# Second attention in another order with two more buffers, and its output projection begun in its last steps

## The reference, cut to what matters

```python
def _swa_sinks(h, w_q, sinks, w_o, k_band, v_band):
    q = (h @ w_q).reshape(B, nc, CHUNK, KV_B, GROUP_B, HEAD_DIM)      # 16 chunks of 64, 16 heads of 64
    s = jnp.einsum('bnqgrd,bnkgd->bngrqk', q, k_band).astype(jnp.float32) / math.sqrt(HEAD_DIM)
    s = s - slopes[...] * dist[...]                                    # 128 keys for each chunk
    m = jnp.maximum(jnp.max(s, axis=-1, keepdims=True), sink)
    e = jnp.exp(s - m)
    denom = jnp.sum(e, axis=-1, keepdims=True) + jnp.exp(sink - m)
    p = (e / denom).astype(v_band.dtype)
    o = jnp.einsum('bngrqk,bnkgd->bnqgrd', p, v_band).reshape(B, S, H_B * HEAD_DIM)
    return o @ w_o
```

## Time and profile before

| | us |
|---|---|
| median of 3 runs | 2517.85 (2514.11 to 2519.14) |
| the profiled execution | 2521.02, span 2519.2 |
| PE busy | 2337.5 (93%) |
| DVE busy | 1536.2 (61%) |
| ACT busy | 1149.7 (46%) |
| POOL busy | 1172.5 (47%) |
| granted clock of PE, mean | 0.966 |

### The profile page before, as it was taken

How to read it: one execution, slowest core, us unless ns; L and a number is a source line. 1 busy time by engine, 2 the same in 40 slices (tenths; PEclk the granted TensorE clock), 3 DMA queues, 4 the chain that set the end, 5 groups by cost and what they waited for, 6 DMA issues and landing times.

```text
span 2519.2 us, 30443 instructions
## 1 busy us (share of the span) xinstructions
PE 2337.5 (93%) x10984; PEld 1932.2 (77%) x10984; DVE 1536.2 (61%) x2470; ACT 1149.7 (46%) x1933; POOL 1172.5 (47%) x1580
## 2 busy tenths in 40 slices
PE   4899999997989999999999898988899999999996
PEld 3778788886867777777778687776678888888884
DVE  4565656557777666666664766773375555444456
ACT  4365665748044333333333566662354333333334
POOL 3411313120646666666666351204356666666660
PEclk9989999999999999999999899978899999999998
DMA  6111211113821333333331321114111111111111
GB/s 259 52 47 34 68 34 54 47 47 102 316 76 58 117 118 114 122 121 118 118 105 57 111 68 40 51 34 175 42 34 51 51 51 51 63 55 52 58 51 67
DMA packets 66007, 206.91 MB, mean 82 GB/s; under 512 B 7345, under 2 KB 7985, under 8 KB 65730
## 3 DMA queue, kind: packets, MB, share of 16 engines
q1 hardware_dynamic: 29760, 109.06, 13.2%
q10 hardware_dynamic: 36098, 95.91, 11.6%
HBM read 186.66 MB, written 16.32 MB: 81 GB/s over the span
## 4 chain that ended last, share of the span: by engine, by line
PE 65%; DVE 14%; ACT 8%; POOL 4%; issue 4%; DMA 4%; ACTq 1%; DVEq 0%; POOLq 0%
PE bank L883 38%; PE bank L620 17%; POOL w_spl L549 2%; DVE X L1889 2%; PE bank L636 1%; POOL w_raw L556 1%; DVE H L1610 1%; PE bank L780 1%; PE bank L754 1%; PE bank L815 1%; PE bank L790 1%; POOL S3f L556 1%; PE bank L816 1%; PE bank L817 1%; DVE cV L1859 1%
## 5 line engine op out<-in xcount | busy, mean ns | idle before, releaser
L883 PE MATMUL bank<-H,w_spl 128*128 128x512 f32 x3744 | 880.6, 393 | 33.3 <-DVE H L1610 14.6
L883 PEld LDWEIGHTS bank<-H,w_spl 128*128 128x128 f32 x3744 | 704.3, 189 | 198.0 <-DVE X L1889 29.4
L549 POOL TENSOR_TENSOR w_spl<-w_raw,w_spl 128x256 fp32r<-128x256 f32 x688 | 544.9, 820 | 443.5 <-ACT w_spl L1358 442.1
L620 PE MATMUL bank<-H,w_spl 128*128 128x512 f32 x2016 | 520.7, 408 | 24.9 <-DVE H L1610 10.7
L883 PE MATMUL bank<-TB,w_spl 128*128 128x512 f32 x2112 | 492.5, 389 | 0.3 <-ACT sU L1373 0.3
L620 PEld LDWEIGHTS bank<-H,w_spl 128*128 128x128 f32 x2016 | 386.5, 197 | 106.4 <-issue 20.6
L883 PEld LDWEIGHTS bank<-TB,w_spl 128*128 128x128 f32 x2112 | 396.2, 188 | 83.4 <-issue 0.9
L1358 ACT ACTIVATE w_spl<-w_raw 128x512 fp32r<-128x512 f32 x328 | 201.9, 628 | 546.7 <-PE bank L883 332.9
L487 POOL TENSOR_TENSOR pace<-one_s 128x1 f32<-128x1 f32 x50 | 13.4, 267 | 737.6 <-PE bank L780 355.8
L1889 DVE SCALAR_TENSOR_TENSOR X<-bank,mods,X 128x1024 f32<-128x1024 f32 x176 | 225.0, 1279 | 34.2 <-PE bank L883 34.2
L1882 DVE TENSOR_TENSOR bank<-bank,sU 128x512 f32<-128x512 f32 x80 | 55.9, 699 | 299.7 <-PE bank L883 299.7
(11 more groups left out here) (171 smaller groups left out, 3186.5 us busy)
## 6 DMA issues: line engine op xcount, KB each, us to landing
w_raw<-in_w_stream SPq DMA_DIRECT2D x184, 512.0 KB, 3.8
ada_raw_f<-in_ada_t ACTq DMA_DIRECT2D x128, 256.0 KB, 2.9
ada_raw_o<-in_ada_t ACTq DMA_DIRECT2D x8, 2048.0 KB, 8.3
ada_raw<-in_ada_t SPq DMA_DIRECT2D x8, 1024.0 KB, 18.6
negF<-scratch_f ACTq DMA_DIRECT2D x16, 512.0 KB, 3.8
X<-in_x_t SPq DMA_DIRECT2D x4, 1024.0 KB, 10.8
X<-in_x_t ACTq DMA_DIRECT2D x4, 1024.0 KB, 8.1
scratch_x<-X ACTq DMA_DIRECT2D x1, 4096.0 KB, 12.6
```

Of the source, the lines that this page charges most:

```text
L549: last = pool.tensor_tensor(block_at(layer, b, 1, q, q + 256), src[:, q:q + 256], block_at(layer, b, 0, q, q + 256).bitcast(F32), ALU.subt ...
L620: last = pe.matmul(dst, stat(k, a), mov(k, b), start=(k == 0 and a + b == 0), stop=(k == KT - 1 and a == 1))
L883: last = pe.matmul(dst, block_at(layer, b, x, k * P, k * P + P), mov(y), start=(start and x + y == 0), stop=(stop and x == 1), skip_group_ ...
```

## The change

`PTB` and `O_stB` get a second buffer each, the store of a pair its own semaphores (`o_outB`), and the parts of a pass are put in another order:

- PE: scores of u, transposes of u-2, values of u-3, query quarter.
- DVE: maxima of u, low part of q, low part of the turned probabilities of u-2, normalising of u-1, output sum of u-3 (was u-4).
- ACT: high part of the turned probabilities, store, output half of u-3, exponentials of u, high part of q.

In the last passes ACT loads pairs back into `Hf`, the low half of H seen as float32 (`load_pair`: pairs 0 to 2 in pass 27, 3 and 4 in 28, 5 in 30, 6 in 33), and makes high parts (`pair_high`); DVE makes the low parts in place (`pair_low`), pair 0 in pass 28 up to pair 5 in pass 33. PE takes the sum over these pairs for the first projection tile in the same passes (`out_first`: k = 0 in pass 30 up to 3 in pass 33, 4 and 5 in 34). Behind the loop come k = 6 of the first tile, k = 0 to 6 of the second, and k = 7 of both (`out_two`). The banks of the projection tiles are swapped for this layer, so that the first tile uses banks that the values don't.

```diff
+PAIR_LOADS = {27: (0, 1, 2), 28: (3, 4), 30: (5,), 33: (6,)}
+PAIR_SPLITS = {28: (0,), 29: (1,), 30: (2,), 31: (3,), 32: (4,), 33: (5,)}
+OUT_BESIDE = {30: (0,), 31: (1,), 32: (2,), 33: (3,), 34: (4, 5)}
+PAIRS_BEHIND = [6, 7]
+OUT_BEHIND = [6]
...
-        PTB = at("PTB", [P, 2, 512], F32R, 182)
+        PTB = [at(f"PTB{i}", [P, 2, 512], F32R, kb) for i, kb in enumerate((182, 200))]
-        O_stB = at("O_stB", [P, S], F32, 190)
+        O_stB = [at(f"O_stB{i}", [P, S], F32, kb) for i, kb in enumerate((190, 204))]
...
+            def out_first(ks):
+                for k in ks:
+                    if k == 0:
+                        pe.wait_ge(w_ready, tile_order(W_OUT_B) + 1)
+                        pe.wait_ge(qB_lo, 16)
+                    pe.wait_ge(o_lo, 8 + k + 1)
+                    out_step(1, 0, k, int(k == 0))
+            def out_two():
+                out_first(OUT_BEHIND)
+                pe.wait_ge(w_ready, tile_order(W_OUT_B + 1) + 1)
+                pe.wait_ge(o_addB, 64)
+                for k in range(KT - 1):
+                    out_step(1, 1, k)
+                out_first([KT - 1])
+                out_step(1, 1, KT - 1, 1)
...
+                if 2 <= u <= 33:
+                    turn_b(u - 2)
                 if u >= 3:
                     values_b(u - 3)
-                if 2 <= u <= 33:
-                    turn_b(u - 2)
                 if u < 27:
                     q_quarter((u + 1) // 4 + 1, (u + 1) % 4)
-            out_proj(1)
+                out_first(OUT_BESIDE.get(u, ()))
+            out_two()
...
+            def load_pair(k):
+                if k == 0:
+                    act.wait_ge(qB_ps, 16)
+                for e in range(2):
+                    act.wait_ge(o_outB[k % 2][e], 16 * (k // 2 + 1))
+                act.dma_start(Hf[:, k, 1], dO[k]).then_inc(ob_in[k], 16)
+            def pair_high(k):
+                act.wait_ge(ob_in[k], 16)
+                nc.scalar.activation(H[:, k, 0], Hf[:, k, 1], ACT.Copy).then_inc(o_hi, 1)
...
+            send_pair(7)
+            for k in PAIRS_BEHIND[:-1][:2]:
+                pair_high(k)
+            load_pair(7)
...
+            for j in range(4):
+                act.dma_start(X[:, 2 * j:2 * j + 2], dX.rearrange("k p s -> p k s")[
+                    :, 2 * j:2 * j + 2]).then_inc(x_in[j], 16)
+            pair_high(7)
...
+            def pair_low(k):
+                dve.wait_ge(o_hi, 8 + k + 1)
+                V_.tensor_tensor(H[:, k, 1], Hf[:, k, 1], H[:, k, 0].bitcast(F32), ALU.subtract).then_inc(o_lo, 1)
```

More of the change, by code:

```diff
@@ L189, in program @@
         H = at("H", [P, KT, 2, S], F32R, 0)
+        Hf = at("Hf", [P, KT, 2, S], F32, 0)
         ada_raw0 = at("ada_raw0", [P, KT, 2, D], F32, 0)
@@ L356, in program @@
         o_in = [sem(f"o_in{i}") for i in range(4)]
+        o_outB = [[sem(f"o_outB{i}{e}") for e in range(2)] for i in range(2)]
+        ob_in = [sem(f"ob_in{k}") for k in range(KT)]
         o_hi = sem("o_hi")
@@ L973, in ffn @@
                 return used[0]
-            out_proj(0)
+            for m in range(8):
+                out_tile(0, m)
             square_sum(1, 1)
@@ L1052, in values_b @@
                     for part in range(2):
-                        last = pe.matmul(bank(4 + u % 2, j * P, j * P + P), v, PTB[:, part, j * P:j * P + P],
+                        last = pe.matmul(bank(4 + u % 2, j * P, j * P + P), v, PTB[u % 2][:, part, j * P:j * P + P],
                                          start=(part == 0), stop=(part == 1))
@@ L1069, in _ @@
                     pe.wait_ge(vs_in, 48)
+                if 2 <= u <= 33:
+                    turn_b(u - 2)
                 if u >= 3:
                     values_b(u - 3)
-                if 2 <= u <= 33:
-                    turn_b(u - 2)
                 if u < 27:
                     q_quarter((u + 1) // 4 + 1, (u + 1) % 4)
-            out_proj(1)
+                out_first(OUT_BESIDE.get(u, ()))
+            out_two()
+            for m in range(2, 8):
+                out_tile(1, m)
             square_sum(3, 1)
@@ L1820, in out_proj @@
                 gc = M_G1 + M_L1 * layer
-                for k in range(8 if layer else 0):
-                    dve.wait_ge(o_hi, 8 * layer + k + 1)
-                    V_.tensor_tensor(H[:, k, 1], O_raw[:, k % 4], H[:, k, 0].bitcast(F32),
-                                     ALU.subtract).then_inc(o_lo, 1)
                 for m in range(8):
@@ L1994, in _ @@
             dve.wait_ge(vs_in, 48)
-            for u in range(36):
-                if u <= 27 and u % 2:
-                    q_low(u // 4 + 1, u % 4 // 2)
+            def pair_low(k):
+                dve.wait_ge(o_hi, 8 + k + 1)
+                V_.tensor_tensor(H[:, k, 1], Hf[:, k, 1], H[:, k, 0].bitcast(F32), ALU.subtract).then_inc(o_lo, 1)
+            for u in range(35):
                 if u < 32:
@@ L2015, in _ @@
                     V_.tensor_scalar(nmB[:, b], mxB[:, b], sink_s[:, hp:hp + 1], -1.0, ALU.max, ALU.mult).then_inc(mB, 1)
+                if u <= 27 and u % 2:
+                    q_low(u // 4 + 1, u % 4 // 2)
+                if 2 <= u <= 33:
+                    v = u - 2
+                    dve.wait_ge(ptB_hi, v + 1)
+                    V_.tensor_tensor(PTB[v % 2][:, 1], bank(2 + v % 2), PTB[v % 2][:, 0].bitcast(F32),
+                                     ALU.subtract).then_inc(ptB_lo, 1)
                 if 1 <= u <= 32:
```

105 lines of the change are left out of this document (47 added, 58 removed).

## The result

The changed kernel takes 2476.8 us (median of 4 runs, 2475.8 to 2480.9), the kernel before beside it 2516.4 (4 runs, 2514.1 to 2519.1): a ratio of 0.9844 with an interval of 0.9826 to 0.9861, or 35 to 44 us less. The sign and the first part of the forecast held. Of the 8.2 us, 4.3 are the last steps and the projection, which gave more than was worked out; these alone would have left it inside the range, at 2480.7. The rest is the base, the clock at the start of the attention, and code that the change leaves alone.

What follows compares the result with a forecast made beforehand. PE was taken as the bound in the steady steps, not fully used because of waits and clock. 2521.02 less 23.0 (steady steps 21.9, start 1.1) less 9.7 (last steps) is 2488.3; median 3.2 lower, 2485; range 2480 to 2497.

Steps and rivals of the forecast that it cites:

- part 2: Step 27 (start T) to projection's end: six pairs' read-back and 24 projection matmuls move into the steps; 9.7 us gain.
- So I expect 1.2 GHz: Last steps, from 27: PE idles up to 2.5 us at a time, so half clock; values end at T+41.4.
- DMA issues on ACT cost 0.64 each: Last steps: each pair-load issue takes ACT 0.64 us; three in step 27, two in 28, one in 30.
- The slack: Odd steady steps: normalised probabilities are ready 5.35 us after step start, PE's transposes want them at 5.8; 0.4 us spare.
- The chain of high part, low part, maxima and exponentials: Last steps: maxima 1.2, exponentials 1.85, high part 1.06, low part 1.25, one after the other, 5.4 us a step.
- rival 1: Last steps: the clock comes back because each has 2.6 us of projection beside small matmuls; time 2481; chance 0.12.
- Pair 6 is there: Behind the last steps: pair 6's low part comes at T+46.8, when PE has finished pair 5.
- The 1.1 us of the start: Attention's start: DVE's maxima of step 1 move ahead of the low part of q; first normalising 1.1 us earlier.
- Rival 2: Steady steps: the transposes' 0.4 us slack fails, odd steps lose 0.7 to 0.9 us; time 2495; chance 0.12.
- Rival 3: Last steps: chain high-low-maxima is 7 us long, or pair 7 lands late; part 2 gives nothing, 2495; chance 0.06.
- Rival 4: Steady steps: late normalising stops all of PE and the clock falls, 7.7 us a step against 5.86; 2552; chance 0.04.
- Rival 5: Whole change: the order doesn't change anything that ends last; gain under 5 us; chance 0.04.

Runs made afterwards that it cites:

- the run with the large memset: Changed kernel plus a DVE memset of 1408 columns ahead of the normalising in steps 3 to 26: 2509.8 us, ratio 0.9974.
- the run with the small memset: Changed kernel plus a DVE memset of 256 columns (0.27 us) ahead of the normalising in steps 3 to 26: 2478.4 us.

## Why the prediction was wrong in the last steps, and where it was right

The steps that failed are two of part 2. "So I expect 1.2 GHz": the clock came back beside the projection's matmuls. "DMA issues on ACT cost 0.64 each": they ran beside the exponentials and delayed them by nothing. The end of the values, forecast at T+41.4, came at T+36.2. Of these 5.2 us, 2.0 had been won by the maxima of step 31 (T+23.9, forecast T+25.85): the six issues up to there were priced at 3.8, and 2.0 of waits for PE that the layout didn't have stand against them. The other 3.2 lie behind these maxima, in a stretch with a clock of 0.72 and not 0.50.

**What bounds, and the steady steps: right.** One step was laid out as 4.93 us of PE and taken as 4.95; it measured 4.96, 24 of them 119.0, as forecast, with no wait that makes a row and the clock at 1.00. The 18.5 us of waits that the prediction says would go reach to 1735 us; 11.3 of them lie in these steps, and the sum used 140.70 us as measured, so nothing hung on it. Without its own order DVE would have cost 5.4 us.

**The slack: right in most steps, used up in six.** The forecast had 0.4 us on an odd step. On the timeline of the changed kernel the normalising from 1596.93 ends at 1597.62 and the transposes start at 1598.01, 0.4 later. But in six of the 24 steps it is not 0.69 us long but 1.08:

```profile
1586.76 1.87 POOL L504 TENSOR_TENSOR w_spl<-w_raw,w_spl 128x256 fp32r<-128x256 f32 x2
...
1586.97 1.08 DVE L2070 TENSOR_TENSOR PB<-PB,rdB 128x512 f32<-128x512 f32 x1
...
1587.20 0.22 PE L1062 MATMUL bank<-KSB,QB 128*128 128x128 f32 x1
...
1588.10 0.44 PE L1073 MATMUL bank<-id_f,PB 128*128 128x128 f32 x2
```

It ends 0.05 us before the transposes, which is the hand-over of the run with the large memset and no margin. PE's rows of the step from 1597.16 show what an unhindered one looks like:

```profile
1597.16 0.22 PE L1062 MATMUL bank<-KSB,QB 128*128 128x128 f32 x1
...
1598.01 0.62 PE L1073 MATMUL bank<-id_f,PB 128*128 128x128 f32 x4
```

There the transposes start 0.84 us behind the first score. In the six steps, here from 1587.20, they start 0.90 to 0.92 behind it, and these steps are 5.03 to 5.06 us long where the other 18 are 4.93. So PE did stand for the normalising, by 0.06 to 0.07 us six times. The longer steps make 0.6 to 0.7 us in all, the difference between 119.0 and 24 x 4.93 = 118.3. A second row tells POOL's side, the split instruction of this line in steps 3 to 26 (ns, min/median/max, first and last start):

```profile
L504 POOL TENSOR_TENSOR w_spl<-w_raw,w_spl x24: 729/736/1178, 1527.2 to 1629.0; 128x256 fp32r<-128x256 f32 x24
```

In the run with the small memset the normalising starts 0.44 us after POOL's first split, not 0.21, and takes 0.85, not 1.08. In both it ends 1.29 us after POOL started: 0.69 of its own behind a wait until POOL + 0.60, near the end of a split of 0.73. And POOL's second split, which starts in that time, takes 1.18, longer by 0.45. So each seems to have stood for the other. By this, what the Trainium skill says in SBUF — State Buffer, section "SBUF: two separate sides", that the two exclude each other for a whole instruction, agrees with the trace in six steps of 24, to within some 0.15 us. Where the prediction erred was in the length of what excludes: it took the mean of 0.82 us in the earlier trace rows, which has such waits in it, where the undisturbed split is 0.73. And it let the wait begin with the normalising at its worst, where POOL had already begun 0.21 us before. The two nearly cancel: 0.39 us were lost in each of the six steps, where some 0.33 were free, 0.38 less the hand-over. That the cost was 0.6 us and not 2.5 is luck: POOL's split had begun 0.21 us ahead of the normalising, in each of the six.

**The last steps: the mechanism right, the size too small.** The forecast had T+125.4 for the end of the projection; it is T+121.1 and T+121.6. By its terms:
- "DMA issues on ACT cost 0.64 each": this step failed. The issues of pass 27 run beside the exponentials that stand ahead of them, on the timeline of ACT:

```profile
1645.27 0.40 ACT L1581 ACTIVATE PB<-PB,nmB 128x128 f32<-128x128 f32 x1
1645.38 0.33 ACTq L1552 DMA_DIRECT2D Hf<-scratch_o  x1
...
1645.80 0.41 ACTq L1552 DMA_DIRECT2D Hf<-scratch_o  x1
...
1646.31 0.39 ACTq L1552 DMA_DIRECT2D Hf<-scratch_o  x1
...
1646.83 0.28 ACT L1583 ACTIVATE esB<-nmB,sink_s 128x4 f32<-128x4 f32 x1
1648.15 0.60 ACT L1565 ACTIVATE PTB<-bank 128x512 fp32r<-128x512 f32 x1 [1.04 <-PE bank L1073]
```

  The exponentials took 1.84 us, as without issues, and ended at T+5.35, not T+7.75. Against that ACT then waited twice for PE, 1.04 and 1.00 us, which the layout didn't have. Net, the maxima of step 29 came at T+12.87, not at 14.6. The trace of before already showed it, at a store whose issues run beside exponentials that start 0.39 us apart as ever:

```profile
1691.01 0.45 ACTq L1528 DMA_DIRECT2D scratch_o<-O_stB  x1
1691.13 0.39 ACT L1544 ACTIVATE PB<-PB,nmB 128x128 f32<-128x128 f32 x1
...
1691.50 0.61 ACTq L1528 DMA_DIRECT2D scratch_o<-O_stB  x1
1691.52 0.39 ACT L1544 ACTIVATE PB<-PB,nmB 128x128 f32<-128x128 f32 x1
```

- The chain of high part, low part, maxima and exponentials: 5.4 us were forecast for a step, and the maxima of steps 29, 30 and 31 come at T+12.87, 18.17 and 23.88, that is 5.3 and 5.7 apart. DVE's rows show the chain, the low part waiting for ACT's high part and the maxima behind it:

```profile
1658.67 1.23 DVE L2034 TENSOR_TENSOR H<-Hf,H 128x1024 fp32r<-128x1024 f32 x1 [0.47 <-ACT H L1556]
1659.93 0.29 DVE L2050 CUSTOM_DVE_ANT_0 PB<-bank,bias_s 128x128 f32<-128x128 f32 x1
...
1663.99 1.62 DVE L2034 TENSOR_TENSOR H<-Hf,H 128x1024 fp32r<-128x1024 f32 x1 [0.45 <-ACT H L1556]
1665.64 0.29 DVE L2050 CUSTOM_DVE_ANT_0 PB<-bank,bias_s 128x128 f32<-128x128 f32 x1
```

- "So I expect 1.2 GHz": this step failed too, from 1661 on (T+19.4), and that was rival 1, to which I gave 12 in 100. It had in its favour the one row of before in which dense matmuls brought the clock back, and against it only rows that had none in them; the second kind says nothing of a mixture. The end of the values was forecast at T+41.4, and at T+37 if the clock came back; it is T+36.2 and 35.1.
- "Pair 6 is there": wrong, first for the same reason. With PE through sooner, it waited 2.54 us for it, where rival 1 said 3. Some 2 us of this wait are ACT's order (the high part behind the last store), which the layout didn't look at. Moving the second tile ahead gives the wait and more, 3.9 to 4.4 us.
- The rest of the projection was forecast at 84.0 us and took 84.9 with this wait in it, so 82.3 without; the slow start was gone with the clock.

5.2 us sooner at the values' end and 0.9 later behind it make the 4.3 us. The total for these steps hid another mistake, which didn't change it: the forecast laid the gain to the pairs alone, where a third or more of it (4.7 to 6.5 of 14.0 to 15.3 us) is the new order's.

**The start and the rest.** The 1.1 us of the start are neither borne out nor refuted. To step 3 the kernels with DVE's new order take 15.6 to 15.9 us in three executions, with a granted clock of 0.89 there, and 16.8 to 17.6 in the other eight, with 0.80 or 0.81; before it was 17.6 and 18.1, with 0.81. At the same clock the gain is 0 to 1.3 us, and most of the 2.1 in the table is clock. The base was one profiled execution whose last stretch was at the long end, 716.6 of 712.5 to 716.6; the forecast took it over, less the 3.2 us to the median. The median of before was itself 1.5 us lower with a fourth run. These are no part of the mechanism, and that they carried the time out of the range is chance.

**The rivals.** Rival 1 came true. Rival 2 did in a small way: the slack failed in six steps, by 0.07 us and not by 0.7 to 0.9. Rival 3: the chain was 5.3 to 5.7 us, not 7. Rival 4's mechanism is real, as 1.23 us more on DVE showed (2509.8 us, of the changed kernel's gain all but 6 us gone). Rival 5 is out.

**The range** ended 0.5 us under rival 1, at 2480. That rival was itself priced on a base and a start that were each some us too high, and on issues that cost more than they do; an end of the range should not stand on the value of one case.

## What to carry to other kernels

Put the matmuls that wait for a small engine's product ahead of the dense ones only if that product is ready by a margin, and work the margin out with the longest duration of that instruction, not with its median, and with the hand-over. Behind a stretch of small matmuls at half clock, count with the clock coming back where dense matmuls stand among them, and then ask who is late next; here it was one high part that stood behind a store in its engine's order, and a different order of two tiles hid it. A difference of 4 us between two profiles of 2500 us is worth nothing until the stages are laid beside a second execution of the same kernel.

## What the runs showed of the hardware

- DMA issues on ACT, queued behind exponentials that had all they needed, ran beside them (0.33 to 0.41 us each) and delayed them by nothing, where four in a row ahead of idle ACT took 2.55 us.
- With matmuls of 128 columns alone, busy 24.1 of 31.0 us, the clock stayed at 1.2 GHz. With 34 dense ones put among them it was 1.00 in the 16 us from 1640 to 1656, in which PE was busy throughout. Whether the dense matmuls or the missing idle time did it, no run here separates:

```profile
1640.00:1656.00 16.00, 16.00 (x109) 14.43 (x109) 14.90 (x55) 13.13 (x48) 2.34 (x6) 1.00 0.58 196
```

- In steps 3 to 26, twelve waits of PE of 0.23 us (2.7 us in all) left the clock at 1.00; twelve waits of 0.9 to 2.0 us (16.2 us in all) went with 0.92, and the 11 of the kernel before, of 0.7 to 1.4 us, with 0.94.
- A normalising (two inputs in SBUF) that began while POOL was in a split took 1.08 us instead of 0.69, and the split that followed 1.18 instead of 0.73, in six steps of 24.
